# Two waits in layer two's first pass and one in layer one's: the same work in another order

## The reference

```
h = concat(meta, x)
z = h @ w_in_a ; q, k, v, gate = split(z)          # layer one, mixer A
y = (sliding_window_softmax(q, k, v) * silu(gate)) @ w_out_a
h = layer_norm(alpha * h + y)
z = h @ w_in_b ; q, k, v, gate = split(z)          # layer two, mixer B
y = (stick_breaking(q, k, v) * silu(gate)) @ w_out_b
h = layer_norm(alpha * h + y) ; return h[16:]
```

## Time and profile before

| | us |
|---|---|
| median of 3 runs | 903.95 (903.6 to 906.25) |
| profiled execution, its own time | 903.57 |
| its span, first to last instruction | 901.8 |
| TensorE busy | 889.6 |
| VectorE busy | 561.8 |
| ScalarE busy | 440.5 |

### The profile page before, as it was taken

How to read it: one execution, slowest core, us unless ns; L and a number is a source line. 1 busy time by engine, 2 the same in 40 slices (tenths; PEclk the granted TensorE clock), 3 DMA queues, 4 the chain that set the end, 5 groups by cost and what they waited for, 6 DMA issues and landing times.

```text
span 901.8 us, 17882 instructions
## 1 busy us (share of the span) xinstructions
PE 889.6 (99%) x7153; PEld 858.6 (95%) x7153; DVE 561.8 (62%) x766; ACT 440.5 (49%) x707; POOL 56.1 (6%) x85
## 2 busy tenths in 40 slices
PE   9999999999999999997999999999999999999997
PEld 9999999999999999997999999999999999988886
DVE  6578667766765867796756464565646355545546
ACT  6556456545555544495444353535444444435421
POOL 1322213211200000000000000000000000000000
PEclk9999999999999999999999999999999999999999
DMA  9775465546432545424453444435353544454622
GB/s 348 234 238 179 160 206 138 171 151 208 134 143 94 197 177 187 145 96 180 156 219 140 164 161 154 171 142 183 140 186 140 186 142 166 156 216 158 233 94 94
DMA packets 25256, 153.06 MB, mean 170 GB/s; under 512 B 3410, under 2 KB 3938, under 8 KB 8708
## 3 DMA queue, kind: packets, MB, share of 16 engines
q1 hardware_dynamic: 21600, 142.19, 43.4%
q0 software_dynamic: 2896, 7.70, 4.4%
q10 hardware_dynamic: 724, 2.66, 0.8%
HBM read 150.36 MB, written 2.18 MB: 169 GB/s over the span
## 4 chain that ended last, share of the span: by engine, by line
PE 92%; DVE 3%; ACT 2%; DMA 1%; issue 1%; SPq 0%; DVEq 0%; ACTq 0%
PE bank L333 66%; PE bank L687 10%; PE bank L492 2%; PE bank L450 1%; DVE w_lo L1073 1%; DMA raw<-chunks 1%; PE bank L629 1%; PE bank L631 1%; PE bank L630 1%; ACT w_hi L768 1%; PE bank L565 1%; PE bank L551 1%; PE bank L592 1%; PE bank L354 1%; PE bank L467 1%
## 5 line engine op out<-in xcount | busy, mean ns | idle before, releaser
L333 PE MATMUL bank<-x_hi,w_hi 128*128 128x272 f32 (+1 forms) x1472 | 425.4, 289 | 5.1 <-DVE x_lo L1342 3.0
L1073 DVE TENSOR_TENSOR w_lo<-raw,w_hi 128x2048 fp32r<-128x2048 f32 x128 | 295.4, 2312 | 204.5 <-ACT w_hi L768 172.0
L333 PE MATMUL bank<-x_hi,w_lo 128*128 128x272 f32 (+1 forms) x1472 | 420.3, 286 | 0.0
L333 PE MATMUL bank<-x_lo,w_hi 128*128 128x272 f32 (+1 forms) x1472 | 420.0, 285 | 0.0
L768 ACT ACTIVATE w_hi<-raw 128x2048 fp32r<-128x2048 f32 x116 | 221.8, 1913 | 154.7 <-PE bank L333 103.0
L333 PEld LDWEIGHTS bank<-x_hi,w_hi 128*128 128x128 f32 x1472 | 277.5, 189 | 7.0 <-DVE x_lo L1342 3.7
L333 PEld LDWEIGHTS bank<-x_lo,w_hi 128*128 128x128 f32 x1472 | 278.1, 189 | 0.0
L333 PEld LDWEIGHTS bank<-x_hi,w_lo 128*128 128x128 f32 x1472 | 277.3, 188 | 0.0
L333 PE MATMUL bank<-og_hi,w_hi 128*128 128x272 f32 x256 | 74.7, 292 | 0.0
L333 PE MATMUL bank<-og_hi,w_lo 128*128 128x272 f32 x256 | 74.1, 289 | 0.0
L333 PE MATMUL bank<-og_lo,w_hi 128*128 128x272 f32 x256 | 73.7, 288 | 0.0
(11 more groups left out here) (228 smaller groups left out, 996.8 us busy)
## 6 DMA issues: line engine op xcount, KB each, us to landing
raw<-chunks SPq DMA_DIRECT2D x128, 1024.0 KB, 4.8
work<-bias_table POOLq DMA_DIRECT2D x8, 512.0 KB, 5.5
work<-chunks SPq DMA_DIRECT2D x4, 512.0 KB, 12.8
work<-bias_table POOLq DMA_DIRECT2D x8, 256.0 KB, 6.8
work<-ln_rows ACTq DMA_DIRECT2D x1, 2048.0 KB, 8.1
out<-work SPq DMA_DIRECT2D x8, 256.0 KB, 2.6
h<-xT SPq DMA_DIRECT2D x2, 544.0 KB, 9.6
raw<-chunks SPq DMA_DIRECT2D x4, 256.0 KB, 5.3
```

Of the source, the lines that this page charges most:

```text
L333: last = mm(o, l, r, start=(kt == 0 and n == 0), stop=(kt == KT - 1 and n == 2))
L1073: V.tensor_tensor(lo_part, raw[:, half, :, :], hi_part.bitcast(f32), ALU.subtract) \
```

## The change

In layer one's pass 1, DVE's split of chunk (Pg + 2, 0) moves from ahead of the gate products to behind them. In layer two's pass 0 three things change: TensorE's gate block waits for two fewer reads (`free_at = P + 2`, q and k read out, not v); ACT's split of chunk (P_B + 3, 0) moves behind `normal(5)` to `normal(7)`; and DVE's `rest(7)` moves ahead of the capping of the scores. No instruction is added or taken away. Passes of both loops stay as they are.

```diff
-                project(P + 3, x_hi, x_lo, SEQ_COLS, between=mid, layer_b=True)
+                project(P + 3, x_hi, x_lo, SEQ_COLS, between=mid, layer_b=True,
+                        free_at=P + 2 if isinstance(i, int) else None)
...
-            split_hi(P_B + 3, 0, True)
             for n in range(5, KT // 2):
                 normal(n)
+            split_hi(P_B + 3, 0, True)
             split_hi(P_B + 3, 1, True)
...
             def body_a(i, last):
                 Pg = P_Q0 + 2 * i
-                split_lo(Pg + 2, 0)
-                if not (isinstance(i, int) and i == 1):
+                first = isinstance(i, int) and i == 1
+                if not first:
+                    split_lo(Pg + 2, 0)
                     gated(Pg - 2, i - 2, 1)
                     gated_lo(i - 2, 1)
                 gates(Pg, i - 1)
                 gated(Pg, i - 1, 0)
+                if first:
+                    split_lo(Pg + 2, 0)
                 row_maxima(i)
...
-            rest(5)
-            rest(6)
+            for n in range(5, KT // 2):
+                rest(n)
...
                 if isinstance(i, int):
-                    rest(7)
                     split_lo(P + 3, 0, True)
```

## The result

The changed kernel took 897.03 us (median of 4 runs, 896.89 to 898.42), the kernel before 903.98 (median of 4, 903.6 to 906.25). The ratio is 0.9921 with a 95% interval of 0.9902 to 0.9940, so it is faster by 7 us, between 5.4 and 8.9. Forecast were 6.2 us and 897.7.

The account below looks back on a forecast made before the run. TensorE, busy 889.6 of 901.8 us, was taken as the bound. 2.55 + 1.53 + 1.68 + 0.41 = 6.17 us off the profiled 903.57 gives 897.4, off the median 897.8; forecast 897.7, range 896.3 to 900.6.

Parts of the forecast that it names:

- Step 1: Layer two's pass 0, v block: x_lo of pairs 5 to 7 comes sooner, pair 7 starts 2.55 us earlier.
- Step 2: Rest of that v block after pair 7: the clock doesn't fall, 3.88 us for 5.41, gaining 1.53 us.
- Step 3: Layer two's pass 0, gate block: with free_at lowered it doesn't wait for v, gaining 1.68 us.
- The rival of the falling clock: Layer two's v block: the clock falls all the same, gain 4.6 us, 899.3 us; chance 0.16.
- Step 4: Layer one's pass 1: TensorE's wait for ACT's copy goes, scores to next block 1.77 us for 2.18, at most 0.41.
- The read-out of q: Layer one's pass 1: ACT's read-out comes 0.4 us later, margin 0.2, covered; otherwise it costs up to 0.41.
- the next wait is close behind: Layer two: block P_B + 3's first split or the softplus is late, giving back 1.5 to 4 us; about 900.5; chance 0.10.
- it doesn't do what it says: Layer two: normals and rests wait for something else, pairs 5 to 7 come as before; 901.5 us; chance 0.07.
- slower: Layer two's next pass: block P_B + 4's chunk comes after TensorE asks, past 435.2 a loss, about 905; chance 0.03.

Follow-up runs that it names:

- e4: The whole change, but DVE's rest(7) stays behind the caps of the scores in layer two's pass 0; 897.94 us, ratio 0.9926 to the kernel before.
- e5: The whole change, but ACT's split of chunk (P_B + 3, 0) stays ahead of normal(5); 899.58 us, ratio 0.9943 to the kernel before.
- e6: The kernel of e1 with 8, 6 and 9 useless matmuls ahead of the waits for pairs 5, 6 and 7; 900.61 us, ratio 0.9953 to before.
- e2: The kernel before with only layer two's new order of ACT and DVE, without the lowered wait or layer one's edit; 903.95 us, ratio 0.9996.
- e1: The kernel before with only the gate block's wait lowered (free_at = P + 2 in pass 0); 902.13 us, ratio 0.9971.
- e9: The changed kernel with pairs outer, output tiles inner in the second half of layer two's first v block; 896.79 us, ratio 0.9919 to before.
- e11: The changed kernel once more, timed beside e9; 897.06 us, ratio 0.9922 to the kernel before.

## Why the prediction was right

- **Step 1 (2.55 us).** Pair 7 started 38.13 us after layer two's first matmul and now starts 35.59 after it: 2.54. The stops left are 0.31 and 0.41 of idle time. e4 and e5 show that both edits are needed for it.
- **Step 2 (1.53).** The rest of the v block takes 412.48 - 408.61 = 3.87 us, for 5.41; 3.88 was forecast. e6 shows the cause. The 1.53 is won only together with step 3: in the kernel before, the copy of v hid it. The rival of the falling clock didn't come, though it did in e2 and e5, where longer stops stayed. That it could not come is not shown: the clock differs between executions of e1 and e5, and of the changed kernel's nine one took 898.42 us, the others 896.7 to 897.4.
- **Step 3 (1.68).** The gate block starts 39.46 us after layer two's first matmul, for 45.22: 5.76 in all, as summed. The low part of its first chunk was done 1.0 us ahead by reckoning. e9 agrees: its v block ended 38.19 us after layer two's first matmul, 1.25 before e11's (39.44), and TensorE then stood 0.20 for it. `tails` had no wait. The last 0.06 of the 5.82 is the gate block's first matmul, no longer the first after a pause.
- **Step 4 (0.41).** The mechanism was right, the size too small. I read the distance from one execution, took it for the kernel's and put 0.41 as the most that could be won. It hangs on when a transfer lands, and the five traces with the old order have 0.41 to 1.14, mean 0.9: four of the five lie above my bound. This is the term that was mis-sized, by about 0.5.
- **What was hidden stayed hidden.** The read-out of q, with a margin reckoned at 0.2 us, caused no stop. The weights' chunks came early enough, and the pass of the loop is 52.00 us.

With 5.8 in layer two and 0.9 in layer one the gain would be 6.7, where 6.95 was measured between the medians and 6.2 forecast. The last 0.2 is well inside the interval and was not traced. Of the rivals, "the next wait is close behind" and "it doesn't do what it says" are refuted by the timeline, and "slower" by the times.

## What to carry to other kernels

Two edits on one path don't add: alone they gave 0.27 and 1.76 us, together 5.82. When one wait goes, the engine runs into the next, and here, for the larger part, each edit alone left a stop after which TensorE's clock fell, for 1.5 us. So follow each engine to its next wait, and reckon with what the stops that are left do to the clock. A cost can also be hidden behind a later wait, as the fall of the clock was before, and show up only when that wait is gone. A wait that hangs on when a transfer lands is to be read from several executions, and where one engine delivers pairs at a slower rate than another wants them, the order of the matmuls can be changed instead of the engines' queues.

## What the runs showed of the hardware

- In the profiled executions the granted clock went to its lower level after stops of 1.09, 0.75 and 1.16 us within 6 us (before), after 1.09 and 0.76 (e5), and after one of 3.82 us, and there about 1 us after TensorE was at work again (e2). It stayed at the upper one after 0.31 and 0.41 (after), 0.31 and 1.17 (e4), and 1.52 alone. These are single executions, and the times of e1 and e5 suggest that the same stops don't bring the fall each time. At the lower level a matmul of 272 columns came every 0.23 us, for 0.126.
- A GpSimd operation on two operands in SBUF more than doubled DVE's time beside it: 1.77 and 1.89 us for 0.72.
